# A decoder trunk on Trainium2: twelve input-projection tiles multiplied slice by slice in float32 beside the modulation, and S5 weights made in the same loop

## The chip, the cores and the metric

The kernel runs on one NeuronCore of a Trainium2 chip. The metric is the device time of one execution in microseconds; a change of it is read from medians over runs on the same chip.

## What is computed

A trunk of two layers over 256 tokens of width 2048. Only the start of a layer matters here: a modulation vector is made from the conditioning vector `c`, the input is normalised and modulated, and one wide projection feeds three groups of heads.

```python
for l in range(DEPTH):                     # DEPTH = 2
    mod = (silu(c) @ w_ada[l] + b_ada[l]).reshape(B, 6, D)
    sh1, sc1, gt1, sh2, sc2, gt2 = ...
    h = rmsnorm(x, g_pre_mix[l]) * (1.0 + sc1) + sh1
    proj = h @ w_in[l]                     # mLSTM, S5 and NSA inputs
    y = concat([mlstm(proj), s5(proj, lam, dt, b, c, d), nsa(proj)]) @ w_out[l]
    x = x + gt1 * rmsnorm(y, g_post_mix[l])
    h = rmsnorm(x, g_pre_ffn[l]) * (1.0 + sc2) + sh2
    x = x + gt2 * rmsnorm(conv_ffn(h), g_post_ffn[l])
```

The S5 group is a diagonal complex state space; its powers and mixing matrices are worked out on the chip from `lam`, `dt`, `b` and `c`, and applied as matrix products.

## The kernel before

The function `trunk` writes one program per engine: SyncE (SP) issues loads, GpSimd (POOL) issues other loads and does some vector work, TensorE (PE) multiplies, ScalarE (ACT) and VectorE (DVE) do the rest. Semaphores tie them. Tokens lie along the free dimension (256), features along the 128 partitions, so h is 16 slices of 128 features, and a projection tile is 128 output columns by 256 tokens.

**Head.** Shift and gain of layer 0's first modulation need 32 chunks of 1 MB of `w_ada` (16 for the shift, then 16 for the gain). SP issues them into five slots borrowed from three tensors (L455 to L460, `head_slot`); VectorE multiplies a chunk with silu(c) and sums it in one instruction (L1709 to L1716). Meanwhile x is loaded, normalised and turned. Twelve dummy matmuls (`keep`, HEAD_KEEP) run near the end of this. Only then come the modulated h, cut into a high and a low half, and the first two tiles (`first_proj`).

**Tiles.** 41 tiles follow in the order of ORDER: tiles 0 to 3 for S5, 4 to 15 keys and values, 16 the gates, 17 to 24 queries, 25 to 32 mLSTM, 33 to 40 values and output gates. Each needs two chunks of 512 KB, which SP loads into `ring`, a ring of five slots shared with other raw weights (compress weights at CMP_TILE, S5 tables at IN_TILE and OUT_TILE). Float32 accuracy is reached by three products of halves: ScalarE rounds a chunk (`w_head`, L1204 to L1206), VectorE subtracts it to get the rest (`w_rest`, L1652) and frees the slot (`raw_free`), and TensorE does 48 matmuls (`proj`, L671), after which ScalarE copies the tile out (`in_tile`, L1341).

```python
for p, (w, h) in enumerate(((w_hi, hT_hi), (w_hi, hT_lo), (w_lo, hT_hi))):
    m = pe.matmul(ps[:, bank, 0:SEQ], w[:, s, ks], h[:, k, :],
                  start=k == 0 and p == 0, stop=k == KT - 1 and p == 2)
```

**S5 weights.** Between the tiles VectorE makes the S5 weights of the layer: `s5_first`, `s5_second`, `s5_powers`, `s5_scaled`, then for each of four groups a block b (at tiles 6, 9, 12, 15, the tuple S5_B) and a block c one tile later. TensorE turns b (`s5_in_weights`) and multiplies c (`s5_own_weights`), and ScalarE sends three tables a group to DRAM (`s_in_w`, `s_out_w`, `s_own_w`); they come back through the ring from tile 18 on. From tile 15 on VectorE also multiplies half-chunks of the next modulation, which POOL loads into `ada_w`.

## Time and profile before

| what | value |
|---|---|
| time of three runs | median 2558.2 us (2551.77 to 2558.7) |
| the profiled execution | 2555.83 us, span 2553.9, granted clock 0.981 |
| busy | PE 2360.3 us (92%), weight loads 2056.5 (81%), DVE 1943.5 (76%), ACT 1304.7 (51%), POOL 262.5 (10%) |
| DMA | 643.07 MB, mean 252 GB/s |
| chain that ended last | PE 70%, DVE 17%, DMA 6%, ACT 4%, issue 2% |

The profile is of one execution. Busy times are sums over the whole span, and the chain is followed back from the last instruction, so its shares say which engine's work set the end. The stretch that the change rewrites is the first 187 us, and its rows are given further down.

### The profile page before, as it was taken

Reading aid. Unit: us, or ns where it says so; the run is one execution under the profiler, and the core shown is the slowest. Engines: PE = TensorE matmul, PEld = TensorE weight load, DVE = VectorE, ACT = ScalarE, POOL = GpSimd, SP = SyncE. Lnnn points to the kernel's source line nnn. Section 1 sums busy time; section 2 is a strip of 40 time slices with the busy share of each in tenths; the row PEclk is TensorE's granted clock in tenths of the full one; section 3 lists DMA queues with packets and bytes.
Section 4 is the critical chain, followed back from the end, with each engine's and each line's share of the span. In section 5 each row is a group of like instructions: output and inputs, shape, how many; then the busy total and the mean of one; then the engine's idle time right before and its main releaser. Section 6 shows DMA issues by size and latency. Waiting matters only on the chain.

```text
span 2553.9 us, 40347 instructions
## 1 busy us (share of the span) xinstructions
PE 2360.3 (92%) x14026; PEld 2056.5 (81%) x14026; DVE 1943.5 (76%) x2791; ACT 1304.7 (51%) x2089; POOL 262.5 (10%) x393
## 2 busy tenths in 40 slices
PE   1689779998999999999988999999899999999998
PEld 0589778766888888888878998887688888888886
DVE  7898887798999988867668976569897565565555
ACT  1565356546455454544448456654554544444444
POOL 0032311110111111100002121001010000000000
PEclk9999889999999999999999999999999999999999
DMA  9859767695999998868764675549596555556564
GB/s 396 328 195 322 268 248 252 221 358 204 354 344 341 334 338 325 318 230 276 263 243 149 226 249 186 141 145 367 207 353 238 184 186 188 183 188 189 190 194 152
DMA packets 187835, 643.07 MB, mean 252 GB/s; under 512 B 27249, under 2 KB 37617, under 8 KB 181697
## 3 DMA queue, kind: packets, MB, share of 16 engines
q1 hardware_dynamic: 120450, 455.28, 49.7%
q0 software_dynamic: 46656, 171.48, 19.5%
q10 hardware_dynamic: 20608, 14.72, 1.8%
q8 instruction: 74, 1.21, 0.2%
q14 instruction: 47, 0.39, 0.0%
HBM read 626.68 MB, written 14.71 MB: 251 GB/s over the span
## 4 chain that ended last, share of the span: by engine, by line
PE 70%; DVE 17%; DMA 6%; ACT 4%; issue 2%; ACTq 0%; SPq 0%; DVEq 0%; POOLq 0%
PE ps L1145 24%; PE ps L688 17%; PE ps L1146 12%; PE ps L671 8%; DVE w_lo L1652 5%; DMA ada_w<-ada_d 3%; DVE mix L1652 3%; DVE ada_w L1658 3%; PE ps L1025 2%; DMA ring<-stream 2%; ACT w_hi L1206 1%; DVE side L1652 1%; DVE mix L1658 1%; DVE mix L1655 1%; DMA s_own_w<-mix 1%
## 5 line engine op out<-in xcount | busy, mean ns | idle before, releaser
L1652 DVE TENSOR_TENSOR w_lo<-ring,w_hi 128x1024 fp32r<-128x1024 f32 x744 | 914.3, 1233 | 483.1 <-ACT w_hi L1206 480.1
L1206 ACT ACTIVATE w_hi<-ring 128x1024 fp32r<-128x1024 f32 x744 | 787.5, 1060 | 871.1 <-PE ps L1146 382.5
L1145 PE MATMUL ps<-hT,w_hi 128*128 128x512 f32 x2688 | 949.7, 399 | 0.5 <-DVE w_lo L1652 0.5
L1146 PE MATMUL ps<-hT,w_lo 128*128 128x256 f32 x2688 | 754.8, 281 | 0.0
L1145 PEld LDWEIGHTS ps<-hT,w_hi 128*128 128x128 f32 x2688 | 505.0, 188 | 126.9 <-DVE w_lo L1652 1.1
L1146 PEld LDWEIGHTS ps<-hT,w_lo 128*128 128x128 f32 x2688 | 507.8, 189 | 0.0
L671 PE MATMUL ps<-hT,w_hi 128*128 128x256 f32 x2496 | 474.7, 292 | 11.0 <-DVE w_lo L1652 11.0
L1658 DVE SCALAR_TENSOR_TENSOR ada_w<-ada_w,cs_row 128x1024 f32<-128x1024 f32 (+1 forms) x334 | 411.6, 1266 | 17.7 <-DMA ada_w<-ada_d 14.6
L671 PEld LDWEIGHTS ps<-hT,w_hi 128*128 128x128 f32 x2496 | 400.3, 197 | 22.7 <-issue 21.4
L671 PE MATMUL ps<-hT,w_lo 128*128 128x256 f32 x1248 | 358.4, 287 | 0.0
L671 PEld LDWEIGHTS ps<-hT,w_lo 128*128 128x128 f32 x1248 | 245.3, 197 | 0.0
L546 POOL DMA_DIRECT2D ada_w<-ada_d x256 | 135.2, 528 | 1067.7 <-DVE ada_w L1658 1062.9
L688 PE MATMUL ps<-w_hi,x_hi 128*128 128x512 f32 x656 | 202.3, 389 | 1.8 <-DVE x_lo L1652 1.8
L688 PE MATMUL ps<-w_hi,x_lo 128*128 128x512 f32 x656 | 202.0, 389 | 0.0
L688 PE MATMUL ps<-w_lo,x_hi 128*128 128x512 f32 x656 | 201.9, 389 | 0.0
L688 PEld LDWEIGHTS ps<-w_hi,x_hi 128*128 128x128 f32 x656 | 123.0, 188 | 27.9 <-DVE x_lo L1652 2.4
L688 PEld LDWEIGHTS ps<-w_lo,x_hi 128*128 128x128 f32 x656 | 123.1, 188 | 25.6
L688 PEld LDWEIGHTS ps<-w_hi,x_lo 128*128 128x128 f32 x656 | 123.1, 188 | 25.5
L636 PE MATMUL ps<-cst,mix 128*128 128x128 f32 x128 | 24.7, 374 | 97.1 <-ACT mix L1307 70.6
L636 PEld LDWEIGHTS ps<-cst,mix 128*128 128x128 f32 x128 | 22.6, 201 | 99.8 <-issue 70.7
L1658 DVE SCALAR_TENSOR_TENSOR mix<-ff_a,aux,mix 128x255 f32 (+3 forms) x172 | 82.8, 482 | 15.1 <-DVE mix L1658 12.2
L1025 PE MATMUL ps<-w_hi,x_hi 128*128 128x512 f32 x224 | 74.2, 413 | 13.5 <-DVE x_lo L1652 12.5
(292 smaller groups left out, 2324.8 us busy)
## 6 DMA issues: line engine op xcount, KB each, us to landing
ring<-stream SPq DMA_DIRECT2D x760, 512.0 KB, 4.4
ada_w<-ada_d POOLq DMA_DIRECT2D x320, 512.0 KB, 6.3
ada_w<-ada_d SPq DMA_DIRECT2D x14, 1024.0 KB, 10.0
ring<-ada_d SPq DMA_DIRECT2D x12, 1024.0 KB, 10.1
mix<-ada_d SPq DMA_DIRECT2D x6, 1024.0 KB, 10.2
xs<-x SPq DMA_DIRECT2D x2, 2048.0 KB, 11.9
s_in_w<-mix ACTq DMA_DIRECT2D x8, 512.0 KB, 3.4
s_out_w<-mix ACTq DMA_DIRECT2D x16, 256.0 KB, 6.6
```

The lines of the kernel that those rows point to most:

```text
L546: pool.dma_start(ada_w[:, s, :], ada_src(u * UG + j // 2, j % 2)).then_inc(ada_full[s], 16)
L636: m = pe.transpose(ps[:, b, k * SEQ + t * P:k * SEQ + (t + 1) * P], xn[:, t, (2 * b + k) * P:(2 * b + k + 1) * P], ident)
L671: m = pe.matmul(ps[:, bank, 0:SEQ], w[:, s, ks], h[:, k, :], start=k == 0 and p == 0, stop=k == KT - 1 and p == 2)
L688: m = pe.matmul(ps[:, 4 * t + 2 * half + b, :], xx[:, xs_, ts_], w[:, s, b * 512:(b + 1) * 512], start=k == 0 and p == 0, stop=False)
L1025: m = pe.matmul(ps[:, 4 * t + 2 * half + b, :], xx[:, j % 2, ts_], w[:, c % SPLIT, b * 512:(b + 1) * 512], start=j % KT == 0 and p == 0, s ...
L1145: pe.matmul(ps[:, bank, :], w_hi[:, s, ks], hT[:, k, :, :], start=k == 0, stop=False)
L1146: m = pe.matmul(ps[:, bank, SEQ:2 * SEQ], w_lo[:, s, ks], hT_hi[:, k, :], start=False, stop=k == KT - 1)
L1206: s.activation(w_hi[:, c % SPLIT, :], ring[:, at % RING, :], ACT.Copy).then_inc(hi_ready, 1)
L1652: return v.tensor_tensor(o, a, b, op)
L1655: return v.tensor_scalar(o, a, s1, s2, op0, op1)
L1658: return v.scalar_tensor_tensor(o, a, s, b, op0, op1, accum_out=total)
```

## The change

In layer 0 alone:

- POOL issues the 32 modulation chunks, into six slots (`ada_w` and the memory of `w_lo` and `w_hi`), shift and gain of a slice alternately, so that slice k of h is complete after chunk 2k + 1.
- SP loads x first, then the weights of tiles 0 to 11 as 24 chunks of 512 KB, each holding four tiles for two slices, in rows of 1 KB. They go through the ring of five slots and are freed by `head_used`.
- ScalarE makes slice k of h as soon as its two chunks are multiplied (`head_h`). TensorE multiplies it raw, in float32, with the twelve tiles of that slice (`head_products`), which are kept in six PSUM banks; all twelve end with slice 15. VectorE makes the low halves (`head_rest`) for the later tiles.
- The S5 weights are made between the chunks (HEAD_B, HEAD_C give the chunk numbers; HEAD_IN, HEAD_OWN the slices after which TensorE does its part), and ScalarE sends the tables after the `head_h` that follows.
- Tiles 12 on are as before, but the compress weights of layer 0 come at tiles 14 to 17, two a tile, instead of 10 to 17. The dummy matmuls, `first_proj` and the halves of tiles 0 to 11 are gone. Layer 1 does what it did.

```diff
-HEAD_UNITS, HEAD_SLOTS = 4, 5
-HEAD_X = 26
+HEAD_UNITS, HEAD_SLOTS = 4, 6
+HT, HW = 12, 4
+HG = HT // HW
+HF = 8
...
+CMP_AT = ([HT + 2 + i // 2 for i in range(N_CMP)], [CMP_TILE + i for i in range(N_CMP)])
...
+        def head_group(n):
+
+            return n // 2 + n % 2 * KT
 
         block = ctx.enter_context(nc.Block())
 
@@ -452,12 +473,7 @@
 
             sp.dma_start(c_row, c_cols.rearrange("(o p) k -> o (p k)", o=1)).then_inc(c_in, 16)
             sp.dma_start(cst[:, 0:K_FIRST], consts[:, 0:K_FIRST]).then_inc(cst_in, 16)
-            for n in range(HEAD_UNITS * UG):
-                if n >= HEAD_SLOTS:
-                    sp.wait_ge(ada_step, 2 * (n - HEAD_SLOTS + 1))
-                sp.dma_start(head_slot(n), ada_rows[n, :, :]).then_inc(head_full[n % HEAD_SLOTS], 16)
-                if n == 2 * HEAD_SLOTS:
-                    sp.dma_start(xs[:, :, :], x.rearrange("b (t p) d -> p (b t) d", p=P)).then_inc(x_in, 16)
+            sp.dma_start(xs[:, :, :], x.rearrange("b (t p) d -> p (b t) d", p=P)).then_inc(x_in, 16)
...
+            def head_src(c):
+
+                kp, g = divmod(c, HG)
+                at, col = C_IN + (ORDER[HW * g] - T_U) % NPROJ * 2, 2 * kp % KH * P
+                return stream[at:at + 2 * HW, :, :].rearrange("(t h) p n -> h p t n", h=2)[2 * kp // KH, :, :, col:col + 2 * P]
...
+            for n in range(HEAD_UNITS * UG):
+                if n >= HEAD_SLOTS:
+                    wait(ada_step, 2 * (n - HEAD_SLOTS + 1))
+                pool.dma_start(head_slot(n), ada_rows[head_group(n), :, :]).then_inc(head_full[n % HEAD_SLOTS], 16)
+                if n == HEAD_SLOTS - 1:
+                    pool.dma_start(cst[:, K_FIRST:], consts[:, K_FIRST:]).then_inc(cst_rest, 16)
...
+            def head_products(k):
+
+                h_hi.wait(pe, 0, k + 1)
+                for j in range(HT):
+                    c = HG * (k // 2) + j // HW
+                    at = RING_SPLIT[0][c]
+                    if k % 2 == 0 and j % HW == 0:
+                        pe.wait_ge(ring_full[at % RING], ring_count(0, at))
+                    bank, off = head_tile(0, j)
+                    o = j % HW * 2 * P + k % 2 * P
+                    m = pe.matmul(ps[:, bank, off:off + SEQ], ring[:, at % RING, o:o + P], h_f[:, k % HF, :],
+                                  start=k == 0 and j % 2 == 0, stop=k == KT - 1 and j % 2 == 1)
+                    if k == KT - 1:
+                        m.then_inc(w_used, 2)
+                    elif k % 2 and j % HW == HW - 1:
+                        m.then_inc(head_used, 1)
...
+                if l == 0:
+                    pe.wait_ge(xt_ready, 8)
+                    s5_b_transposes()
+                    for k in range(KT):
+                        head_products(k)
+                        if k in HEAD_IN:
+                            s5_in_weights(HEAD_IN.index(k))
+                        if k in HEAD_OWN:
+                            s5_own_weights(HEAD_OWN.index(k))
...
+                def head_h(k):
+
+                    s.wait_ge(ada_step, 4 * (k + 1))
+                    s.activation(sh_col[:, k:k + 1], head_sum[:, k:k + 1], ACT.Identity, bias=ada_b_c[:, k:k + 1]).then_inc(sh_ready, 1)
+                    s.activation(modA[:, k:k + 1], head_sum[:, KT + k:KT + k + 1], ACT.Identity, scale=A("g_pre_mix", k, k + 1),
+                                 bias=b_gain[:, k:k + 1]).then_inc(sh_ready, 1)
+                    if k >= HF:
+                        s.wait_ge(head_used, HG * ((k - HF) // 2 + 1))
+                        h_lo.wait(s, 0, (k - HF) // 2 + 1)
+                    s.wait_ge(sh_ready, 2 * (k + 1))
+                    s.activation(h_f[:, k % HF, :], xT[:, k, :], ACT.Identity, bias=sh_col[:, k:k + 1], scale=modA[:, k:k + 1])
+                    h_hi.by(s.activation(hT_hi[:, k, :], xT[:, k, :], ACT.Identity, bias=sh_col[:, k:k + 1], scale=modA[:, k:k + 1]))
...
+                    for k in range(KT):
+                        head_h(k)
+                        if k == 0:
+                            s5_b_columns()
+                        if k == 1:
+                            s5_skips()
+                        if k - 1 in HEAD_IN:
+                            in_weights(HEAD_IN.index(k - 1))
+                        if k - 1 in HEAD_OWN:
+                            out_weights(HEAD_OWN.index(k - 1))
+                            own_weights(HEAD_OWN.index(k - 1))
+                    for c in range(2 * HT, 2 * HT + AHEAD):
+                        w_head(c, used=False)
+                    for n in range(HT):
+                        if n == HF:
+                            h_lo.wait(s, l, 8)
+                        in_tile(n)
...
+                    for n in range(HEAD_UNITS * UG):
+                        head_chunk(n)
+                        if n == 2:
+                            for t in range(TT):
+                                rstd.wait(v, l, t + 1)
+                                v.reciprocal(stat[:, 4 + t:5 + t], stat[:, 2 + t:3 + t]).then_inc(x_root, 1)
+                        if n == 3:
+                            s5_first()
+                        if n == 7:
+                            s5_second()
+                        if n == 8:
+                            s5_powers()
+                        if n == 9:
+                            s5_scaled()
+                        if n >= 8 and n % 4 == 0:
+                            head_rest(n // 4 - 2)
+                        if n in HEAD_B:
+                            s5_weights_b(HEAD_B.index(n))
+                        if n in HEAD_C:
+                            s5_weights_c(HEAD_C.index(n))
+                    head_rest(6)
+                    head_rest(7)
+                    h_tmp.given += 8 - len(H_BY_ACT)
+                    v.sem_inc(h_tmp.sem, 8 - len(H_BY_ACT))
...
+HEAD_B, HEAD_C = (10, 15, 21, 26), (13, 19, 24, 29)
+HEAD_IN, HEAD_OWN = (6, 9, 11, 14), (8, 10, 13)
```

How the order of instructions changes, first on VectorE, around the S5 block c of the second group. `apow` are the S5 powers, `w_lo<-ring,w_hi` the low half of a weight chunk, `s5_own` TensorE's own-weights product and `st_out` the landed table. Before, between tiles:

```order
L1652 TENSOR_TENSOR w_lo<-ring,w_hi 128x1024 [waits hi_ready] x2
L1652 TENSOR_TENSOR mix<-aux,apow 128x640 [waits st_out,s5_own]
L1652 TENSOR_TENSOR side<-aux,apow 128x640 [waits dve]
L1652 TENSOR_TENSOR mix<-mix,side 128x640 [waits dve]
L1652 TENSOR_TENSOR mix<-aux,apow 128x640 [waits dve]
L1652 TENSOR_TENSOR side<-aux,apow 128x640 [waits dve]
L1652 TENSOR_TENSOR mix<-mix,side 128x640 [waits dve]
L1652 TENSOR_TENSOR w_lo<-ring,w_hi 128x1024 [waits hi_ready] x2
```

The block stands between the low halves of two tiles, and waits for `st_out` and `s5_own` there.

After, on the same engine, in the chunk loop (`ada_hi`, `ada_w`, `ada_lo` are slots of modulation chunks, `head_sum` their sums):

```order
L1792 SCALAR_TENSOR_TENSOR ada_hi,head_sum<-ada_hi,cs_row 128x2048 [waits head_full4]
L1786 TENSOR_TENSOR hT<-mix,hT 128x2x256 [waits h_hi]
L1792 SCALAR_TENSOR_TENSOR ada_hi,head_sum<-ada_hi,cs_row 128x2048 [waits head_full5]
L1792 SCALAR_TENSOR_TENSOR ada_w,head_sum<-ada_w,cs_row 128x2048 [waits head_full0]
L1792 SCALAR_TENSOR_TENSOR ada_w,head_sum<-ada_w,cs_row 128x2048 [waits head_full1]
L1786 TENSOR_TENSOR mix<-aux,apow 128x640 [waits st_out,s5_own]
L1786 TENSOR_TENSOR side<-aux,apow 128x640 [waits dve]
L1786 TENSOR_TENSOR mix<-mix,side 128x640 [waits dve]
L1786 TENSOR_TENSOR mix<-aux,apow 128x640 [waits dve]
L1786 TENSOR_TENSOR side<-aux,apow 128x640 [waits dve]
L1786 TENSOR_TENSOR mix<-mix,side 128x640 [waits dve]
L1792 SCALAR_TENSOR_TENSOR ada_lo,head_sum<-ada_lo,cs_row 128x2048 [waits head_full2]
```

The same block, with the same two waits, now stands in front of the remaining modulation chunks, and `hT` (the low half of h) among them.

ScalarE after, from slice 9 of h to the tables of the first group (`sh_col` and `modA` are the shift and gain of a slice):

```order
L1376 ACTIVATE sh_col<-head_sum,ada_b_c 128x1 [waits ada_step]
L1377 ACTIVATE modA<-head_sum,b_gain,aux 128x1
L1383 ACTIVATE mix<-mix,sh_col,modA 128x256 [waits sh_ready,h_lo,head_used]
L1384 ACTIVATE hT<-mix,sh_col,modA 128x256
L1477 DMA s_out_w<-mix 128x4x128 [waits s5_pow]
L1477 DMA s_out_w<-mix 128x4x128
L1489 ACTIVATE mix<-ps 32x4x32 [waits s5_zero,s5_own]
L1489 ACTIVATE mix<-ps 32x4x64
L1489 ACTIVATE mix<-ps 32x4x96
L1489 ACTIVATE mix<-ps 32x512
L1492 DMA s_own_w<-mix 128x512 [waits s5_own_ev]
```

The two issues of `s_out_w` and the own weights stand behind `head_h` of the next slice, which waits for its two chunks (`ada_step`), where before they stood behind a tile's evacuation.

The queue that issues the modulation chunks, before (SyncE, at the head):

```order
L453 DMA mix<-c_cols 1x2048
L454 DMA cst<-consts 128x261
L458 DMA ada_w<-ada_d 128x2048 x2
L458 DMA ring<-ada_d 128x2048 x2
L458 DMA mix<-ada_d 128x2048
L458 DMA ada_w<-ada_d 128x2048 [waits ada_step] x2
L458 DMA ring<-ada_d 128x2048 [waits ada_step] x2
L458 DMA mix<-ada_d 128x2048 [waits ada_step]
```

Each chunk behind the fifth waits for a multiplication (`ada_step`).

And after (POOL, which had only the small tables here before):

```order
L575 DMA posi<-pos 128x256
L576 DMA aux<-aux_d 128x64
L578 DMA mix<-ada_b 128x128
L579 DMA mix<-ada_b 64x128
L580 DMA aux<-aux_d 128x2642
L584 DMA ada_w<-ada_d 128x2048 x2
L584 DMA ada_lo<-ada_d 128x2048 x2
L584 DMA ada_hi<-ada_d 128x2048 x2
L586 DMA cst<-consts 128x1340
L584 DMA ada_w<-ada_d 128x2048 [waits ada_step,c_in] x2
```

The first chunk stands behind the tables and before the rest of the constants; the seventh waits for the first multiplication (`ada_step`).

SyncE now begins with x and the first five weight chunks, and its later loads up to tile 13 wait for TensorE (`head_used`, `w_used`).

## Rows read from the trace of the kernel before

In the windows view a row holds the stretch and its length, then busy us and count of PE, PEld, DVE, ACT and POOL, then the granted clock, the DMA share and GB/s. In the groups view: busy us, mean ns, then the idle time before them.

**Rows 1.** Windows view, three stretches of the start.
```profile
12.66:93.22 80.56, 10.08 (x51) 9.30 (x52) 72.87 (x66) 12.50 (x19) 1.09 (x2) 1.00 1.01 418
114.45:185.90 71.45, 64.36 (x539) 63.40 (x537) 63.40 (x101) 44.26 (x71) 21.24 (x20) 0.98 0.56 186
186.00:273.00 87.00, 74.36 (x692) 71.25 (x692) 71.06 (x88) 43.91 (x72) 16.62 (x18) 0.92 0.84 304
```

**Rows 2.** Chain of waits: start us, us, what; from 28, 114 and 245 us.
```profile
28.27 12.52 DMA ada_w<-ada_d
...
114.69 17.29 PE ps L671 x144
...
245.51 19.39 DMA s_own_w<-mix
```

**Rows 3.** DMA view, 12 to 80 us, total.
```profile
DMA packets 3890, 28.45 MB, mean 418 GB/s; under 512 B 417, under 2 KB 417, under 8 KB 417
```

**Rows 4.** Groups by form, 88 to 94 us: a chunk multiplication and the dummy matmuls.
```profile
L627 PE MATMUL ps<-cst 128*128 128x256 f32 x24 | 5.4, 383 | 1.4 <-DVE mix L1658 1.4
L1658 DVE SCALAR_TENSOR_TENSOR ada_w<-ada_w,cs_row 128x2048 f32<-128x2048 f32 x2 | 4.6, 2292 | 0.4 <-DMA ada_w<-ada_d 0.4
```

**Rows 5.** Timeline of PE, from 186 and from 273 us.
```profile
186.24 0.64 PE L817 MATMUL ps<-ring,side 128*32 128x128 f32 x16 [1.44 <-DMA ring<-stream]
...
273.04 0.58 PE L671 MATMUL ps<-hT,w_hi 128*128 128x256 f32 x1
```

**Rows 6.** Windows view: S5 first part, powers, scaled, a block b, a block c.
```profile
117.37:120.58 3.21, 3.21 (x29) 3.21 (x28) 2.76 (x18) 1.15 (x2) 0.00 (x0) 1.00 0.81 257
135.30:141.87 6.57, 6.57 (x57) 6.57 (x56) 5.89 (x21) 6.44 (x11) 2.56 (x2) 1.00 0.26 85
145.26:152.20 6.94, 3.99 (x34) 3.78 (x32) 6.77 (x7) 6.18 (x11) 6.54 (x8) 1.00 0.31 108
178.84:183.16 4.32, 4.32 (x38) 4.32 (x37) 4.15 (x8) 0.00 (x0) 0.00 (x0) 1.00 0.99 348
185.35:190.47 5.12, 4.23 (x46) 4.03 (x47) 4.95 (x8) 3.20 (x6) 0.00 (x0) 1.00 0.82 314
```

**Rows 7.** Groups by form, 93 to 300 us.
```profile
L1206 ACT ACTIVATE w_hi<-ring 128x1024 fp32r<-128x1024 f32 x52 | 55.2, 1062 | 50.9 <-DMA ring<-stream 29.8 <-PE ps L671 20.2 <-PE ps L656 0.8
...
L1287 ACT ACTIVATE hT<-ps,mod,modA 128x256 fp32r<-128x256 f32 x16 | 8.8, 611 | 0.0
...
L1652 DVE TENSOR_TENSOR hT<-mix,hT 128x512 fp32r<-128x512 f32 x8 | 5.3, 689 | 0.2
```

**Rows 8.** DMA view, 375.6 to 377.7 us: one load with 1 KB rows.
```profile
q1 hardware_dynamic: 528, 0.52, 80.2%
```

**Rows 9.** DMA view, 160 to 270 us: the queue of the S5 tables.
```profile
q10 hardware_dynamic: 5888, 5.24, 14.0%
```

**Rows 10.** View of the tile s_out_w, all executions of its issue.
```profile
DMA to landing us min/median/max: 2.7/5.8/20.1
```

**Rows 11.** The page, costliest groups and DMA issues (KB each, us to landing).
```profile
L546 POOL DMA_DIRECT2D ada_w<-ada_d x256 | 135.2, 528 | 1067.7 <-DVE ada_w L1658 1062.9
...
ring<-stream SPq DMA_DIRECT2D x760, 512.0 KB, 4.4
ada_w<-ada_d POOLq DMA_DIRECT2D x320, 512.0 KB, 6.3
```

**Rows 12.** Timeline of ACT: evacuations of tiles 17, 18 and 19.
```profile
231.21 0.38 ACT L1341 ACTIVATE mix<-ps 128x256 f32<-128x256 f32 x1
...
238.60 0.38 ACT L1341 ACTIVATE mix<-ps 128x256 f32<-128x256 f32 x1
...
249.22 0.38 ACT L1341 ACTIVATE mix<-ps 128x256 f32<-128x256 f32 x1
```

**Rows 13.** Windows view, just after the wait for s_own_w.
```profile
268.10:276.80 8.70, 8.66 (x39) 8.09 (x40) 8.60 (x10) 0.45 (x2) 2.63 (x4) 0.50 0.53 166
```

More of the change, by code:

```diff
@@ L110, in _ring_places @@
         for n in range(NRAW):
-            if min(2 * RAW_TILE[n] + 4, S_OUT - 1) == c:
+            if min(2 * tile[n] + 4, S_OUT - 1) == c:
                 raw.append(at)
@@ L387, in joint_parts, with raw, head_tile @@
             return slice(a, m), slice(m, D)
-        def raw(n):
-            return ring[:, RING_RAW[n] % RING, :]
+        def raw(l, n):
+            return ring[:, RING_RAW[l][n] % RING, :]
+        def head_tile(l, n):
+            return (n // 2, n % 2 * SEQ) if l == 0 and n < HT else (n % 2, 0)
         def modw(n):
@@ L1311, in _, with head_scaled, head_turned @@
-                h_evac(0, {4: 2, 6: 3} if l == 0 else {})
+                if l:
+                    h_evac(0, {})
+                def head_scaled(t):
+                    s.wait_ge(x_root, t + 1)
+                    for i in range(XN_PARTS):
+                        part = slice(i * D // XN_PARTS, (i + 1) * D // XN_PARTS)
+                        xn_ready.by(s.activation(xn[:, t, part], xs[:, t, part], ACT.Identity, scale=stat[:, 4 + t:5 + t]))
+                def head_turned(b):
+                    h_tr.wait(s, 0, b + 1)
+                    s.activation(xT[:, 2 * b:2 * b + 2, :].rearrange("p a b -> p (a b)"), ps[:, b, :], ACT.Copy
+                                 ).then_inc(xt_ready, 1)
```

333 lines of the change are left out of this document (185 added, 148 removed).

## Prediction

> **What bounds the kernel now.** I read the busy shares by stretch first, then the chain of waits, then the DMA view. In the first 93 us the DMA engines are full (share 1.01, 418 GB/s), while VectorE is busy 72.87 of 80.56 us and TensorE 10.08 [rows 1]. The chain says the same: each pair of modulation chunks is followed by some 10 us on the queue behind it [rows 2]. 28.45 MB went through in 68 us at 418 GB/s [rows 3], so a 1 MB chunk (1.049 MB) costs 2.51 us of DMA, and one multiplication on VectorE 2.29 us [rows 4]: the transfer bounds by a little. From 114 to 273 us VectorE (63.40 of 71.45, then 71.06 of 87.00) and TensorE (64.36, 74.36) share the stretch, and DMA has room [rows 1]. Tile 12 follows the raw matmuls that start at 186.24, and tile 21 starts at 273.04 [rows 5]. Between them lies one bare wait, 19.39 us for the S5 table `s_own_w`, written too shortly before [rows 2]. The change does the work up to tile 12 in another order; from tile 21 on the program is the same, so the question is when those two tiles begin.
>
> **The new head, on VectorE.** It now carries four things in one line, and I sum them.
> Start: x (2.1 MB), the large table (1.3 MB) and the first chunk must land, and the weight chunks queued beside them take about as much as the chunk and half of x; 5.5 MB at 418 GB/s [rows 3] is 13 us from issues at about 2: 15 (before, the first multiplication is at 12.66, where that stretch starts [rows 1]).
> Chunks: 32 × 2.29 = 73.3 [rows 4].
> S5 weights: the first part 3.2, powers 6.6, scaled 6.9, each b block 4.3, each c block 5.1 [rows 6]; the second part has 12 small operations against 18 in the first, 2.1; one memset 0.5. 3.2 + 2.1 + 6.6 + 6.9 + 0.5 + 4 × 4.3 + 4 × 5.1 = 56.9.
> Low halves of h: 8 × 0.69 = 5.5 [rows 7].
> Together 150.7. Against it stand the others. TensorE: 12 float32 matmuls of the slice's shape take 5.4 us (24 records) [rows 4], 16 slices 87, and at most 18 for the S5 transposes and own weights (20 matmuls a group, none dearer than these at 0.227). DMA: 32 × 2.51 = 80; a weight chunk now has 1 KB rows, and the one load of that kind took 80.2% of 2.1 us = 1.68 [rows 8], 24 of them 40; x and tables 10; S5 writes 14.0% of 110 us = 15 for four blocks, 11.5 for three [rows 9]. That is 142, below 151, so VectorE is the longest.
> Waits that the sum does not hold: early chunks that arrive late, 4 (the five weight loads stand in the same engines); and the S5 blocks. Block b of the second group waits for TensorE's transposes of the first, 4. Blocks c of groups two to four wait for `st_out`, the landing of the table of the group before. ScalarE issues it only behind `head_h` (two large activations of 0.61 [rows 7] and two small ones, 1.7), which itself waits for the chunk just multiplied. 1.7, two issues of about 0.5 and a landing between 2.7 and 5.8 [rows 10]: 5 to 8; I take 6, 5 and 7 for the three. Behind a c block on VectorE stand all later chunks, so this is paid in full, and the queue of chunks fills meanwhile for nothing. The bounds are 0 (all landed) and 20.1 each [rows 10]; I take the median since the DMA queues are far from full here. 150.7 + 4 + 4 + 18 = 176.7.
>
> **Chunks from POOL's queue.** Before, SP issued them; now POOL does, behind two small tables and the large one, with six slots. POOL's issues of the same tensor take 528 ns with VectorE beside them, and 512 KB lands 6.3 us later [rows 11]; six slots cover 5 × 5.5 = 27 us of the line on VectorE, so nothing is added. The Trainium skill speaks against the move: its page "SBUF — State Buffer" (section "SBUF: two separate sides") says that descriptors which GpSimd builds wait while VectorE holds the port that the two share; the 528 ns speak against it for these operations, and its outcome is a rival below.
>
> **From the head to tile 12.** After the last chunk: `head_h` 1.7. Then slice 15, which frees the three last weight slots; the loads of tiles 12 and 13 land 4.4 us after issue [rows 11], w_hi takes 1.06 twice [rows 7] and w_lo follows, while ScalarE also evacuates the first tiles. Slice 15 up to its first third 2, load 4.4, two w_hi and a w_lo 3.3, and 0.6 of issue: 10.3. Tile 12 starts at 176.7 + 12.0 = 189, where the raw matmuls before it started at 186.24 [rows 5]. So all the tile products taken out, and the splitting of their weights, buy nothing up to here: VectorE does nearly the same number of microseconds.
>
> **Tiles 12 to 20.** Before: 273.0 − 186.9 = 86, with the 19.39 in it. Now the S5 tables were written 20 us and more before they are loaded (own group four apart, at tile 12, loaded from tile 22 on). The wait goes. What is late next: two tiles without extra work at 5.8 (three tiles took 17.29 [rows 2]) and seven at the pace of 231.21 to 238.60, 7.4 [rows 12]; with the last own weights 3: 11.6 + 51.8 + 3.2 = 67. Eight compress chunks now come two per tile at tiles 14 to 17, in a ring of five; at 2.1 to 4.4 us a load I count them inside 7.4. Tile 21 starts at 189 + 67 = 256 against 273.0, gain 17. Removing the twelve dummy matmuls gives nothing, they hid behind the chunks. The modulation halves from tile 15 on are unchanged. Layer 1 is the same. The sum is against the profiled execution, 2555.8: **2539 us**. The median of the runs is 2.4 higher, so this is read with that much slack. A measurement here tells about 0.3% (7.7 us) from nothing.
>
> **Rivals.**
> *No waits in the head.* If the tables land in the shadow of a chunk, the 22 of waits and the 4 at the start vanish: 151, tile 12 at 160 with a shorter tail, tile 21 at 227, **2509**. For it: the writes are small and the DMA has room. Against: the order on ScalarE puts the issue behind the chunk after which VectorE asks.
> *The wait is only replaced.* The compress chunks take two of five slots each tile, every tile then waits for its weights as tile 18 to 19 did, 10.6 [rows 12]: 11.6 + 7 × 10.6 = 86, tile 21 at 275, **2558**.
> *Late filling.* Each of the six issues that fill the slots stands behind a VectorE operation as long as a chunk's, 6 × 2.29 = 14 later at the start: **2553**. This is where the rule of "SBUF — State Buffer" would lead. Against: POOL's issues last 528 ns [rows 11].
> *Slower: TensorE at half clock.* TensorE gets 5.4 us of work each 11 us. After the 19.39 us wait the granted clock was 0.50, the 1.2 GHz level, for 8.70 us, though it was busy [rows 13]. A slice at that level costs 10.9; from about 40 (x has to be scaled, turned and copied first) 16 × 10.9 = 174, S5 18, end 4: tile 12 at 236, tile 21 at 303, **2586**. It decides once a slice costs more than (177 − 40 − 18)/16 = 7.4. Against: a slice of 5.4 raises the clock again while it runs, then it costs between the two. The Trainium skill, "TensorE: Matmul & The Clock Gate" (section "HAM oscillation — how this bites in real kernels"), tells of a loop whose every burst starts slow because it waits before each; by that this rival would be nearer than I put it, and the row shows 0.50 after a far longer wait only.
> *Slower: the table writes land late.* At 19.4 each [rows 2] instead of 5.8, three times 13.6 = 41: **2580**. The writes have short rows and stand beside full queues of chunks, which speaks for it; the median speaks against.
>
> **Numbers.** Forecast 0.54, no waits 0.19, replaced 0.11, late filling 0.03, half clock 0.07, late landings 0.06. Faster: 0.52 of the forecast, 0.19, and 0.01 of the replaced wait, 0.72. Same: 0.02, 0.10 and 0.03, 0.15. Slower: 0.13. The range goes from 2506 (the first rival with 3 to spare) to 2562 (the replaced wait with 4); the two slow rivals, 0.13, stay out.
>
> **What would show it.** The first modulation multiply at about 15 and the last at about 177; the 128x640 group on VectorE preceded by waits on the `s_out_w` DMA of 5 to 7, three times; a slice's twelve matmuls in 5.4 at clock 1.00; tile 12 at 189, tile 21 at 256; no wait of 19 for `s_own_w`. Wrong it would be if TensorE's slices show clock 0.50 through the head, or if VectorE waits for chunks in the middle of it.

## The result and the profile after

The median of 20 runs is 2561.0 us against 2555.1 for the kernel before (20 runs); the ratio is 1.0031, with a 95% interval of 1.0016 to 1.0046. The change makes the kernel slower by 0.3%. The forecast was 2539 with a chance of 0.72 for faster. The direction was wrong, and that the median still lies in the forecast range is luck: tile 21 starts 30.9 us later than the sum has it, and the range was wide enough only because of a rival whose mechanism no run shows (below).

VectorE's timeline in the head: start us, us, operation, and in brackets the idle time before it and what ended it. The first multiplication, the first operation of each S5 block that waits, and the last multiplication:

```profile
16.65 2.29 DVE L1792 SCALAR_TENSOR_TENSOR ada_w<-ada_w,cs_row 128x2048 f32<-128x2048 f32 x1 [2.81 <-DMA ada_w<-ada_d]
...
94.71 0.69 DVE L1786 TENSOR_TENSOR mix<-aux,apow 128x512 f32<-128x512 f32 x1 [13.34 <-PE ps L792]
...
118.56 0.82 DVE L1786 TENSOR_TENSOR mix<-aux,apow 128x640 f32<-128x640 f32 x1 [10.08 <-DMA s_out_w<-mix]
...
149.33 0.82 DVE L1786 TENSOR_TENSOR mix<-aux,apow 128x640 f32<-128x640 f32 x1 [9.15 <-DMA s_out_w<-mix]
...
178.13 0.82 DVE L1786 TENSOR_TENSOR mix<-aux,apow 128x640 f32<-128x640 f32 x1 [7.79 <-DMA s_out_w<-mix]
...
185.38 2.29 DVE L1792 SCALAR_TENSOR_TENSOR ada_w<-ada_w,cs_row 128x2048 f32<-128x2048 f32 x1
```

The four waits that the forecast named are there, in the places it named, but they are 40.4 us and not 22. The last multiplication ends at 187.7, not 177.

Tile 12 and tile 21 on TensorE (the first and the last line, to be compared with [rows 5]), and between them the compress product that waits:

```profile
201.07 0.58 PE L693 MATMUL ps<-hT,w_hi 128*128 128x256 f32 x1 [3.96 <-ACT mix L1414]
...
233.72 1.08 PE L858 MATMUL ps<-ring,side 128*32 128x128 f32 x16 [4.55 <-DMA ring<-stream]
...
286.88 0.58 PE L693 MATMUL ps<-hT,w_hi 128*128 128x256 f32 x1
```

Tile 12 comes 12.1 us later than forecast and the nine tiles take 85.8 instead of 67, so tile 21 starts 13.8 us later than before. The long wait for `s_own_w` of [rows 2] is gone, as forecast, but nothing of its 19.39 us was gained: the nine tiles took 86.2 us before and take 85.8 now.

Windows view of the changed kernel, columns as in [rows 1]:

```profile
16.60:39.70 23.10, 7.84 (x43) 7.22 (x44) 19.55 (x34) 18.95 (x36) 3.70 (x7) 0.94 1.02 412
63.64:81.00 17.36, 17.36 (x72) 14.96 (x73) 17.16 (x18) 3.33 (x8) 2.11 (x4) 0.89 0.99 359
92.80:118.60 25.80, 19.86 (x91) 16.79 (x90) 13.64 (x16) 6.11 (x14) 2.11 (x4) 0.83 0.77 264
149.30:189.60 40.30, 21.49 (x104) 18.05 (x104) 30.73 (x35) 9.43 (x23) 0.53 (x1) 0.76 0.39 127
201.00:287.00 86.00, 75.66 (x645) 72.56 (x645) 59.24 (x61) 52.04 (x91) 37.99 (x38) 0.86 0.81 290
```

Up to 81 us the DMA engines are full (share 1.02 and 0.99); over the longer stretches behind that they are not (0.77 and 0.39). TensorE's granted clock is lower on average once its work comes in pieces (0.83, 0.76, 0.86, where the kernel before had 0.98 and 0.92 in [rows 1]). And GpSimd is busy 38 us in the last stretch against 16.6 before. The queues from 16 to 64 us (packets, MB, share of 16 engines):

```profile
q0 software_dynamic: 2285, 16.25, 82.3%
q1 hardware_dynamic: 3245, 3.22, 20.0%
```

Modulation chunks (q0) took four fifths of the DMA time, and the weights that TensorE waited for (q1) got 3.22 MB in 48 us.

### The profile page after: what moved, and what is told of

Same layout as the page of the kernel before. It is cut to its first block, busy times and chain, and to the rows that moved or that the text cites. A ratio compares the mean times of both kernels' runs of the same rounds, so it can differ in the third digit from the quotient of the medians.

```text
span 2557.1 us, 39914 instructions
## 1 busy us (share of the span) xinstructions
PE 2382.6 (93%) x13810; PEld 2069.2 (81%) x13810; DVE 1907.8 (75%) x2756; ACT 1297.5 (51%) x2116; POOL 278.7 (11%) x425
## 4 chain that ended last, share of the span: by engine, by line
PE 72%; DVE 14%; DMA 6%; ACT 5%; issue 2%; SPq 1%; ACTq 0%; DVEq 0%; POOLq 0%
PE ps L1202 24%; PE ps L710 17%; PE ps L1203 12%; PE ps L693 9%; DVE w_lo L1786 4%; DMA ring<-stream 3%; DVE ada_w L1792 3%; PE ps L1082 3%; DVE mix L1786 2%; ACT w_hi L1263 2%; PE ps L759 1%; DMA s_out_w<-mix 1%; DMA ada_w<-ada_d 1%; DVE side L1786 1%; DVE mix L1792 1%
## 5 line engine op out<-in xcount | busy, mean ns | idle before, releaser
L1786 DVE TENSOR_TENSOR w_lo<-ring,w_hi 128x1024 fp32r<-128x1024 f32 x720 | 888.7, 1238 | 493.3 <-ACT w_hi L1263 489.0
L1263 ACT ACTIVATE w_hi<-ring 128x1024 fp32r<-128x1024 f32 x720 | 761.3, 1059 | 837.1 <-PE ps L1203 348.2
L1203 PE MATMUL ps<-hT,w_lo 128*128 128x256 f32 x2688 | 753.8, 280 | 0.0
L1202 PEld LDWEIGHTS ps<-hT,w_hi 128*128 128x128 f32 x2688 | 504.1, 188 | 118.8 <-DVE w_lo L1786 0.9
L1203 PEld LDWEIGHTS ps<-hT,w_lo 128*128 128x128 f32 x2688 | 508.5, 189 | 0.0
L693 PE MATMUL ps<-hT,w_hi 128*128 128x256 f32 x2176 | 418.2, 294 | 9.4 <-DVE w_lo L1786 5.5
L693 PEld LDWEIGHTS ps<-hT,w_hi 128*128 128x128 f32 x2176 | 352.5, 199 | 20.9 <-issue 15.0
L693 PE MATMUL ps<-hT,w_lo 128*128 128x256 f32 x1088 | 314.2, 289 | 0.0
L693 PEld LDWEIGHTS ps<-hT,w_lo 128*128 128x128 f32 x1088 | 215.5, 198 | 0.0
L710 PE MATMUL ps<-w_hi,x_hi 128*128 128x512 f32 x656 | 202.4, 390 | 1.8 <-DVE x_lo L1786 1.8
L759 PE MATMUL ps<-mix,ring 128*128 128x256 f32 x384 | 102.9, 434 | 48.9 <-ACT hT L1384 38.7
L759 PEld LDWEIGHTS ps<-mix,ring 128*128 128x128 f32 x384 | 83.5, 221 | 66.1 <-ACT hT L1384 31.6
L1792 DVE SCALAR_TENSOR_TENSOR mix<-ff_a,aux,mix 128x255 f32 (+3 forms) x172 | 82.9, 482 | 15.1 <-DVE mix L1792 12.2
L1731 ACT ACTIVATE mix<-ff_a,aux 128x256 f32 (+1 forms) x86 | 51.1, 594 | 75.2 <-DVE ff_a L1786 75.0
## 6 DMA issues: line engine op xcount, KB each, us to landing
ada_w<-ada_d POOLq DMA_DIRECT2D x12, 1024.0 KB, 10.4
ada_lo<-ada_d POOLq DMA_DIRECT2D x10, 1024.0 KB, 11.6
```

The costliest lines, as they stand in the source:

```text
L693: m = pe.matmul(ps[:, bank, 0:SEQ], w[:, s, ks], h[:, k, :], start=k == 0 and p == 0, stop=k == KT - 1 and p == 2)
L710: m = pe.matmul(ps[:, 4 * t + 2 * half + b, :], xx[:, xs_, ts_], w[:, s, b * 512:(b + 1) * 512], start=k == 0 and p == 0, stop=False)
L759: m = pe.matmul(ps[:, bank, off:off + SEQ], ring[:, at % RING, o:o + P], h_f[:, k % HF, :], start=k == 0 and j % 2 == 0, stop=k == KT - 1 ...
L1202: pe.matmul(ps[:, bank, :], w_hi[:, s, ks], hT[:, k, :, :], start=k == 0, stop=False)
L1203: m = pe.matmul(ps[:, bank, SEQ:2 * SEQ], w_lo[:, s, ks], hT_hi[:, k, :], start=False, stop=k == KT - 1)
L1263: s.activation(w_hi[:, c % SPLIT, :], ring[:, at % RING, :], ACT.Copy).then_inc(hi_ready, 1)
```

## The experiments

All times of tiles and chunks are from one profile of each kernel; ratios are to the kernel before on the same chip, with 95% intervals. Two profiles of one and the same kernel differ by 0.3 to 1.6 us at tile 12 and by 1.5 to 1.8 at tile 21 (the last experiment), so smaller differences between two kernels say nothing.

**Tables issued earlier (a_out).**

```diff
+                        if k in HEAD_OUT:
+                            out_weights(HEAD_OUT.index(k))
                         if k - 1 in HEAD_OWN:
-                            out_weights(HEAD_OWN.index(k - 1))
...
+HEAD_OUT = (7, 10, 12)
```

> The two issues of s_out_w move ahead of the own weights and up to two slices earlier on ScalarE (behind head_h of slices 7, 10 and 12). Theory 1 (VectorE's c blocks wait for the landing of that table, 10.1, 9.2 and 7.8 us in the changed kernel): the second and third wait nearly vanish, the first falls only to the end of TensorE's own weights (some 2 us less, since slice 8 ends late), so the last chunk ends some 11 to 14 us earlier than 187.6 and tile 12 starts at about 188. Rival (the landing only looks last, the blocks wait for TensorE's own weights all the same): waits stay at 8 to 10, last chunk within 3 us of 187.6. Whole time 10 lower, or unchanged.

Ratio 0.9990 (0.9965 to 1.0014). The last chunk ends at 182.2 and tile 12 starts at 195.3. Waits view of VectorE, head (total us, times, longest):

```profile
DVE mix L1787 <- PE ps L792: 14.3, 1, 14.3
DVE mix L1787 <- PE ps L810: 12.4, 2, 7.9
DVE mix L1787 <- DMA s_out_w<-mix: 8.4, 1, 8.4
```

The last chunk ends 5.5 us earlier, half of what was expected. Two of the three waits for the table now end with TensorE's own weights (L810), 7.9 and 4.4, which the table had hidden; the third is still for the table. So both theories hold in part: the issue order costs 5.5 us, and behind it stands TensorE. In this profile both passes of the up projection are of the shorter kind described in the last experiment.

**Second b block later (b_late).**

```diff
-HEAD_B, HEAD_C = (10, 15, 21, 26), (13, 19, 24, 29)
+HEAD_B, HEAD_C = (10, 17, 21, 26), (13, 19, 24, 29)
```

> Block b of the second group comes after chunk 17 and not after chunk 15. Theory 1 (it waits 13.3 us for TensorE, which is behind because its weight chunks arrive late, while modulation chunks lie ready in the slots): VectorE multiplies two more chunks in that time, its wait falls from 13.3 to about 8, last chunk about 5 us earlier, unless the first c block waits longer in its place. Rival (the DMA queues are full until 92 us, so nothing that VectorE does earlier helps): the wait shrinks but the same time comes back as a wait for chunks or in the next blocks; last chunk still at 187 within 2.

Ratio 1.0031 (1.0009 to 1.0053). The wait shrinks from 13.3 to 12.2 only, the last chunk ends at 187.3, tile 12 starts at 201.0: the rival. TensorE's transposes end 3.9 us later (98.6 against 94.7), and TensorE waits 14.7 us for its weights in the head where it waited 10.2, so the two chunks that VectorE does ahead of them gain nothing.

**Contiguous weight rows (e_rows).** The rows are 4 KB instead of 1 KB. This multiplies other weights in tiles 0 to 11, so the output is not the trunk's; the work is the same.

```diff
-                return stream[at:at + 2 * HW, :, :].rearrange("(t h) p n -> h p t n", h=2)[2 * kp // KH, :, :, col:col + 2 * P]
+                return stream[c, :, :].rearrange("p (t n) -> p t n", t=HW)
```

> The 24 weight chunks of tiles 0 to 11 are read as contiguous chunks with 4 KB rows and not as 1 KB rows; this multiplies other weights, so tiles 0 to 11 hold other numbers (the work is the same). Theory 1 (1 KB packets take turns with 8 KB packets of the modulation chunks and so get a small share while those stream): TensorE's waits for the ring in the head (10 us in three waits, and the wait before slice 0) go, slices 0 to 6 end before 80 us and block b of the second group waits 4 instead of 13.3; last chunk about 9 us earlier. Rival (the DMA is simply full, 418 GB/s, whatever the rows): TensorE's waits stay, last chunk within 3 us of 187.6.

Ratio 1.0006 (0.9981 to 1.0031). VectorE's waits in the head:

```profile
DVE mix L1786 <- DMA s_out_w<-mix: 33.6, 3, 14.0
DVE ada_w L1792 <- DMA ada_w<-ada_d: 6.1, 2, 4.7
```

The wait for TensorE's transposes (13.3) is gone altogether, so late weights had made it, and with 4 KB rows they are hardly late (TensorE waits 1.8 us for the ring and not 10.2). But the waits for the table grew from 27.0 to 33.6, and only 3.7 us reach tile 12 (197.3). Up to 64 us the weights got no more than before (3.38 MB against 3.22); from 64 to 78 us they got 1.86 MB against 1.27, and the transposes end at 83.5 and not 94.7.

**Both moves (c_both).**

```diff
+HEAD_B, HEAD_C = (10, 17, 23, 27), (13, 20, 25, 30)
+HEAD_IN, HEAD_OWN = (6, 9, 12, 14), (8, 11, 13)
+HEAD_OUT = (7, 10, 12)
```

> Both moves together: tables issued early, second b block after chunk 17, third after 23, fourth after 27, c blocks after 13, 20, 25 and 30, TensorE's parts moved with them. Theory 1 (the four waits of VectorE, 40.4 us in all, are set by TensorE's lateness and the issue order): they fall to 10 or less, the last chunk ends at 157 to 162, tile 12 starts at about 173, and the whole is 15 to 28 us below the changed kernel, so clearly below the kernel before. Rival (the waits move to the modulation chunks or to TensorE, whose slices then bound): last chunk at 175 or later, whole within 8 of the changed kernel.

Ratio 0.9965 (0.9941 to 0.9989), median 2544.4: below the kernel before, and 1.0031 to 0.9965 is 17 us. So the waits in the head decided the direction. Both passes of the up projection in its profile take 475 us (see the last experiment), as in the kernel before, and still a span of 2546.7 us against 2553.9. The last chunk ends at 170.2 and not at 157 to 162, tile 12 starts at 182.5. Two long waits are left, 13.1 for TensorE's transposes and 8.4 for a table whose two writes, issued at 122.5 and 123.0, had landed at 141.2: together 21.5 where theory 1 had 10 or less. It is theory 1 in the main, with less than it promised.

**First b group turned earlier (g_early).** As before, with

```diff
+HEAD_B, HEAD_C = (10, 17, 23, 27), (13, 20, 26, 30)
+HEAD_IN, HEAD_OWN = (5, 9, 12, 14), (8, 11, 13)
+HEAD_OUT = (7, 10, 13)
```

> Like the run with both moves, but TensorE turns the first b group after slice 5 and not after slice 6, and the third c block comes after chunk 26. Theory 1 (VectorE's 13.1 us there are TensorE waiting for the weight chunks of slices 6 and 7, which the modulation chunks crowd out): the wait goes and VectorE works on; last chunk at 157 to 161 instead of 170.2. Rival (the DMA queues are full until 92 us, so VectorE then waits for modulation chunks or for ScalarE in the next block): last chunk at 166 to 171. Whole 8 to 12 us lower than the run with both moves, or within 4 of it.

Ratio 0.9938 (0.9904 to 0.9973), median 2540.9 of five runs; the interval overlaps that of c_both, and its one profile starts tile 12 later than c_both's (185.4 against 182.5). The waits view:

```profile
DVE mix L1787 <- PE ps L810: 17.1, 1, 17.1
DVE mix L1787 <- DMA s_out_w<-mix: 9.0, 1, 9.0
```

The 13 us went and came back as 17 at the next block that needs TensorE; the last chunk ends at 173.1, where theory 1 had 157 to 161 and the rival 166 to 171. So the rival's kind of outcome came, but the wait moved to TensorE and not to chunks or ScalarE. TensorE is late as a whole there, not in one place.

**Contiguous rows on top (j_rows).** This is g_early with the edit of e_rows, so tiles 0 to 11 hold other numbers again.

> The kernel with the earlier first b group, with the weight chunks of tiles 0 to 11 read contiguously (4 KB rows; other weights, so tiles 0 to 11 hold other numbers, same work). Theory 1 (what is left of VectorE's waits there, 17.1 us for TensorE's own weights of group one, is late weight chunks in 1 KB packets): the wait falls to 5 or less, the last chunk ends at 158 to 163 instead of 173.1. Rival (TensorE itself, its clock and its place in the order, makes that wait): it stays above 10, last chunk at 168 or later.

Ratio 0.9962 (0.9945 to 0.9979).

```profile
DVE mix L1787 <- DMA s_out_w<-mix: 21.7, 2, 13.4
...
DVE ada_lo L1793 <- DMA ada_lo<-ada_d: 2.8, 2, 1.5
```

TensorE's own weights of group one are done at 100 us, 14 earlier, so the part of theory 1 on the rows holds; but the block then waits 13.4 for the first table, issued at 84.7 and 85.1. The view of that table's writes, all of them in the run (the longest is this one):

```profile
DMA to landing us min/median/max: 2.6/4.7/28.8
```

The last chunk ends at 171.6 and not at 158 to 163. Taking one wait away shows the next: at this one block it was 17.1 us for TensorE and is 13.4 for the table.

**Blocks moved two or three chunks further (m_best).**

```diff
+HEAD_B, HEAD_C = (10, 17, 24, 28), (13, 22, 27, 31)
+HEAD_IN, HEAD_OWN = (5, 9, 12, 14), (8, 11, 13)
+HEAD_OUT = (7, 11, 13)
```

> The kernel with the earlier first b group, with the second c block after chunk 22 and not 20, the third after 27, the fourth after the last chunk, the third and fourth b blocks after 24 and 28. Theory 1 (VectorE's 17.1 and 9.0 us there are waits for work that would be done anyway two or three chunks later): both shrink below 5, the last chunk ends at 152 to 160 instead of 173.1, and tile 12 starts 10 to 18 us earlier than 185.4. Rival (slices on TensorE and the DMA queues bound the head by now): the waits move to the chunks or to slice 15, tile 12 within 5 us of 185.4.

Ratio 0.9957 (0.9941 to 0.9974), median 2546.8. The last chunk ends at 165.8 and tile 12 starts at 181.2, 4.2 earlier than in g_early; one c block now comes behind the last chunk. The 17 us stay (17.3), only later, and the 9.0 for the table falls to 4.6: the rival in the main. TensorE waits 20.1 us for its weights in the head here, 21.7 in g_early. The three versions c_both, g_early and m_best beat both kernels, and these runs don't tell which of them is best.

**Filler on TensorE (f_fill, h_fill).** Eight matmuls by zeros behind each of slices 6 to 14, and eight behind slice 15, on the changed kernel and on g_early.

```diff
+                        if 6 <= k < KT - 1:
+                            for _ in range(8):
+                                pe.matmul(ps[:, 0, 0:SEQ], nul[:, :], cst[:, 0:SEQ], start=False, stop=False)
...
+                    for _ in range(8):
+                        pe.matmul(ps[:, 7, 0:SEQ], nul[:, :], cst[:, 0:SEQ], start=True, stop=True)
```

> The changed kernel with eight matmuls by a zero tile (3.6 us at full clock, they add nothing) behind each slice from 6 to 14 and eight behind slice 15. Theory 1 (TensorE falls to the 0.50 clock in the gaps between slices, and slices 8, 10, 12, 15 and tile 12 run 1.3 to 3 us long): granted clock in 92 to 190 us rises from about 0.8 to above 0.95, these slices take 5.5, tile 12 takes 6.0 and starts 2 to 4 us earlier than 201. Rival (the clock is off the path, the filler only stands in front of the S5 products that VectorE waits for): tile 12 starts at 201 or later by up to 5.

> The previous kernel with the zero matmuls. Theory 1: with the waits of VectorE gone TensorE's slices are closer together and matter more, so the filler brings 3 to 6 us up to tile 12. Rival: TensorE is now nearly full (16 slices of 5.5 and the S5 products from 40 us on), and the filler delays it: tile 12 3 to 10 us later than without.

Windows of h_fill, and of g_early for the same stretches:

```profile
92.00:150.00 58.00, 56.92 (x286) 49.80 (x287) 31.86 (x36) 11.16 (x26) 4.22 (x8) 0.97 0.82 304
150.00:190.00 40.00, 38.99 (x207) 34.22 (x206) 28.72 (x32) 14.69 (x31) 0.00 (x0) 1.00 0.44 141
```

```profile
92.00:150.00 58.00, 45.62 (x216) 38.03 (x216) 31.50 (x36) 11.03 (x26) 4.22 (x8) 0.88 0.83 303
150.00:190.00 40.00, 27.02 (x130) 23.27 (x131) 28.80 (x32) 17.70 (x39) 1.65 (x2) 0.83 0.51 172
```

The clock does rise (0.88 and 0.83 to 0.97 and 1.00; from 0.82 and 0.76 to 0.92 and 0.91 on the changed kernel), tile 12 takes 6.0 us instead of 7.3 and 7.5, and it brings nothing: tile 12 starts at 202.8 and 188.5, 1.7 and 3.1 later than without, the 1.7 being hardly more than two profiles of one kernel differ by. By tile 21 the two are even with their bases (285.7 against 286.9, 273.3 against 273.1). The ratios are 1.0043 (1.0019 to 1.0067) and 1.0003 (0.9982 to 1.0024). So the filler costs about as much as the clock gives: the rivals.

**Compress chunks spread (i_cmp), on g_early.** The first product now also waits until the twelve tiles are copied out.

```diff
+CMP_AT = ([HT + 1, HT + 1, HT + 2, HT + 3, HT + 3, HT + 4, HT + 4, HT + 5], [CMP_TILE + i for i in range(N_CMP)])
```

> The kernel with the earlier first b group, and the eight compress chunks at tiles 13, 13, 14, 15, 15, 16, 16, 17 and not two at each of 14 to 17. Theory 1 (two extra loads per tile in a ring of five make TensorE and ScalarE wait for the ring: 4.6 us before the compress of tile 16 and the drop of the clock behind it): that wait falls below 1.5, and tiles 12 to 20 take 79 or less where they took 83 to 86. Rival (the stretch is bound by ScalarE's evacuations, the S5 table loads and the clock): 83 to 86 again.

Ratio 0.9994 (0.9973 to 1.0014). Tile 12 at 188.1 to tile 21 at 277.2 is 89.1, g_early has 87.7: the rival's outcome. It is a weak test: the chunks move by one tile at most, and a product now waited 8.6 us for ScalarE instead.

**Half-chunks of the next modulation later (k_ada), on g_early.**

```diff
-ADA_SLOT = 15
+ADA_SLOT = 20
```

> The kernel with the earlier first b group; the half-chunks of the next modulation begin at tile 20 and not at tile 15 (denser afterwards). Theory 1 (tiles 14 to 20 are short of DMA: two compress loads a tile, the tiles' own, the half-chunks and the S5 tables, share 0.98 and 1.01 there): tile 21 starts 6 to 12 us after tile 12 sooner than the 87.7 us of the base, the loads land in about 4 and not 6 us; part of it comes back behind tile 21. Rival (five ring slots freed late by ScalarE and VectorE bound it, not the transfer): 84 to 90 again.

Tile 12 to tile 21 is 186.6 to 265.6, 79.0 instead of 87.7, and the loads of the S5 tables land in 4.4 instead of 7.8 us. The amount is theory 1's, but the run does not show that DMA alone is the cause: it takes 6.3 MB of loads out of the stretch, and with them the 14 half-chunk multiplications of 1.22 us on VectorE, some of which are in the chain that ends at tile 21 (3.52 us of it, shown below for the changed kernel). The ratio is 0.9981 (0.9965 to 0.9997) against 0.9938 (0.9904 to 0.9973), so nothing of the 8.7 us is seen in the whole: the up projection, which follows the mixer, starts at 627.5 against 618.0. The half-chunks have to be done somewhere, and in these two profiles they cost more there.

**GpSimd's preparation of the compress blocks left out (l_noblk), on g_early.** The eight additions that fill the blocks are left out in layer 0, so the blocks are zero there and the output is not the trunk's.

```diff
-                    pool.memset(blk_all[:, kv, :, 2 * NC:CW], 0.0)
-                    for h in range(NKV):
+                    if l == 0:
+                        b = pool.memset(blk_all[:, kv, :, :], 0.0)
+                    else:
+                        pool.memset(blk_all[:, kv, :, 2 * NC:CW], 0.0)
+                    for h in range(NKV if l else 0):
```

> The kernel with the earlier first b group, leaving out in layer 0 the eight additions on GpSimd that prepare the compress blocks (they become zero). Theory 1 (GpSimd's work, which now comes in one piece behind the twelve evacuations, slows VectorE's operations beside it: 2.26 us for a low half against 1.23): the low halves in the first 25 us behind tile 12 take 1.3 to 1.6 us, and tile 21 starts 4 to 8 us earlier after tile 12. Rival (the slow operations are off the path there): the operations are faster, but tile 21 starts within 2 us of the 87.7 after tile 12.

Groups of VectorE's low halves from 185 to 215 us, in g_early and then in this kernel:

```profile
L1787 DVE TENSOR_TENSOR w_lo<-ring,w_hi 128x1024 fp32r<-128x1024 f32 x7 | 12.9, 1867 | 9.3 <-ACT w_hi L1263 9.3
```

```profile
L1790 DVE TENSOR_TENSOR w_lo<-ring,w_hi 128x1024 fp32r<-128x1024 f32 x7 | 9.8, 1403 | 15.1 <-ACT w_hi L1266 15.1
```

Tile 12 to tile 21 takes 78.1 (186.6 to 264.7), 9.6 less than in g_early, and the up projection starts 7.8 earlier (610.2 against 618.0). The low halves there are 3.1 us shorter together (12.9 to 9.8), and VectorE's other operations in those 30 us 4.3 (10.4 to 6.1). That is theory 1, and more than it promised; how the rest comes about was not tried. The step from tile 15 to tile 16 alone falls from 14.6 us to 7.2, with the same compress loads. Ratio 0.9949 (0.9926 to 0.9971), whose interval does not separate it from g_early's: the profile shows the gain, the medians don't.

**Both kernels once more (after_again, before_again).**

> The changed kernel once more, for a second profile. Theory 1 (a pass of the up projection takes 466 or 475 us by the execution, whatever the kernel, and hides or adds 9 us each time): its head is within 1 us of the first profile at tile 12 (201.1) and tile 21 (286.9), while one of the two passes may differ by 8.7. Rival (the faster first pass belongs to the changed kernel): first pass 466 again, second 475 again.

> The kernel before once more, for a second profile. Theory 1: tile 21 at 273 within 1, and at least one pass of the up projection may take 466 where both took 475. Rival: both 475 again.

The matmuls of the up projection from 700 to 900 us, in the first profile of the changed kernel and in the second:

```profile
L1202 PE MATMUL ps<-hT,w_hi 128*128 128x512 f32 x578 | 200.4, 391 | 0.0
```

```profile
L1202 PE MATMUL ps<-hT,w_hi 128*128 128x512 f32 x568 | 200.7, 399 | 0.0
```

Tile 12 is at 200.8 and tile 21 at 285.4 in the second profile, within 0.3 and 1.5 us of the first: the head repeats, a little less closely at tile 21 than expected. The first pass of the up projection took 466.2 us in the first profile and 475.9 in the second (from the start of its first matmul to the start of its last), of the same kernel. So one program can have either, by the execution: theory 1 for the changed kernel. In the kernel before all four passes of the two profiles took 475, the outcome that its rival named; tile 12 was at 186.8 and 188.4 and tile 21 at 273.0 and 274.9. Whether the kernel before ever has the faster pass is not shown: in the other 14 profiles 8 of 28 passes were of that kind, and with such a share four of 475 in a row are no surprise. The spans of the second profiles are 2564.9 and 2561.2.

## Why the prediction was wrong, step by step

**Start.** Forecast 15, measured 16.65. The rival of a late filling did not occur: POOL's issues take 0.53 us in the head too. I had drawn this rival from "SBUF — State Buffer" of the Trainium skill (section "SBUF: two separate sides") too widely. The section has the building of descriptors locked out while VectorE runs an operation in a two-port mode; an operation with two SBUF inputs it sets only against GpSimd operations that read SBUF. The chunk multiplications have two SBUF inputs, so its rule does not lead to this rival, and the issues beside them took no longer than elsewhere.

**VectorE's own work.** Forecast 73.3 + 56.9 + 5.5 = 135.7; measured 187.7 − 16.65, less 40.4 and 3 of small waits for chunks, 127.6. It was 8 too dear. The S5 weights took 52.3 instead of 56.9, the chunks 71.2 instead of 73.3 (back to back one begins 2.21 us after the other), and two of the eight low halves of h come behind the last chunk. Nearly all that the S5 weights saved is in two steps whose rows had GpSimd beside them [rows 6]: the powers took 6.6 with GpSimd busy 2.56 us and now take 4.4, the scaled step took 6.9 with GpSimd busy 6.54 and now takes 4.3:

```profile
53.25 2.87 DVE L1786 TENSOR_TENSOR mix<-aux,s5p 128x512 f32<-128x512 f32 x4
...
56.15 0.69 DVE L1786 TENSOR_TENSOR aux<-mix 128x512 f32<-128x512 f32 x1
56.88 0.69 DVE L1792 SCALAR_TENSOR_TENSOR aux<-mix 128x512 f32<-128x512 f32 x1
```

**Waits in the head: this step failed.** The mechanism was named rightly, the sizes not. (a) "Block b of the second group waits for TensorE's transposes of the first, 4" was 13.3. The DMA sum (142 in 177 us) was used as an average; up to 81 us the engines are full, and from 16 to 64 us the packets of the chunks' queue took 82.3% of their time. TensorE waited for the ring at 54.7, 63.6 and 90.3 us (10.2 in all) and began the transposes at 92.8 only; e_rows takes that wait away. (b) "6, 5 and 7" for the tables were 10.1, 9.2 and 7.8. A c block waits for both writes of a table, and the second write of the three landed 8.8, 10.6 and 6.5 us after its issue. The landing had been taken at 5.8, the median over both writes and both layers, "since the DMA queues are far from full here". That premise was wrong. The windows view of the three landings, with the DMA share in the last column but one:

```profile
109.65:118.47 8.82, 8.82 (x51) 7.51 (x50) 0.00 (x0) 2.35 (x6) 0.00 (x0) 0.87 0.84 326
138.59:149.23 10.64, 8.35 (x56) 7.41 (x56) 1.58 (x3) 2.28 (x6) 0.53 (x1) 1.00 1.03 368
171.56:178.04 6.48, 6.48 (x45) 5.65 (x45) 0.00 (x0) 2.29 (x6) 0.00 (x0) 1.00 0.98 300
```

The slots that VectorE has just freed are refilled beside the first two (64.3% and 70.1% of the engines' time for the chunks' queue), weights beside the third (62.2%). The kernel before could have told: the second writes of its four groups in layer 0 landed after 6.7, 6.6, 12.4 and 20.1 us. (a) and (b) are together 40.4 us instead of 22, which minus the 8 above and with the later start gives 187.7 instead of 177. c_both, which shortens them to 21.5, is faster than the kernel before.

**From the last chunk to tile 12.** 13.4 instead of 12.0: slice 15 ran 7.5 us and not 5.4, at a granted clock of 0.74 from 187 to 201 us, behind 8.6 us of idle TensorE. This is the rival of the half clock, and it came in part. Four slices from 92 us on followed 5.9, 7.9, 11.6 and 8.6 us of idle TensorE, and took 8.4, 8.0, 7.7 and 7.5 us at a mean granted clock of 0.64 to 0.72, between the levels of 1.2 and 2.4 GHz; slices that followed on work took 5.3 to 5.5 at 0.97 to 1.00. "TensorE: Matmul & The Clock Gate" of the Trainium skill (section "HAM oscillation — how this bites in real kernels") tells of a loop whose every burst starts slow because it waits before each, and for the four slices the trace agrees. It is worth 2 to 3 us in such a slice, and these four are as long as the 7.4 us from which the prediction let the clock decide; but TensorE was idle before each of them, waiting for h, and f_fill, which raises the clock, brings tile 12 no earlier. So it did not bound the head.

**Tiles 12 to 20: this step failed most.** 85.8 instead of 67. I counted nine tiles at the pace of the kernel before and took the wait of 19.39 off; the sum had no term for the work that the first twelve tiles hand on to GpSimd. The rival "the wait is only replaced" gave 86, but that is luck: it had the compress loads as the cause, and l_noblk has the same loads and takes 78.1. What filled the place is read from the chain of waits of the changed kernel (start us, us, what), between tiles 12 and 21:

```profile
219.42 6.71 DVE w_lo L1786 x3
...
226.52 9.80 DMA ring<-stream
...
256.08 5.46 DMA ring<-s_in_w
...
275.80 3.52 DVE ada_w L1792 x6
```

(a) GpSimd's work. Rotations and compress blocks of twelve tiles became due at once (GpSimd busy 38 us, 16.6 before), and VectorE beside it slowed; its low halves free the ring slots late, and the load behind them holds up the compress product and the tile behind it. l_noblk gets 9.6 back. (b) The half-chunks of the next modulation, whose loads stand beside those of the S5 tables and whose multiplications stand on VectorE: k_ada gets 8.7 back, and does not tell the two apart. (a) and (b) overlap in tiles 18 and 19, so they are not a sum. (c) The clock was lower too, 0.86 against 0.92; what that costs in these tiles was not tried by itself.

**Behind tile 21** the program was taken as unchanged, and it is. From tile 21 to the end it took 2280.9 and 2286.4 us in the two profiles of the kernel before, 2270.2 and 2279.5 in those of the changed one. Without the two passes of the up projection, counted to the end of their last matmul, that is 1330.3 and 1335.2 against 1328.3 and 1327.9. So in the profiles tile 21 is 12.2 us later on average and the rest a little shorter, which fits the smaller difference of the medians, 5.9 us; what makes the rest shorter is open, and two profiles of each are too few to say that it is.

Measured against its own sum: 12.1 late at tile 12, 18.8 more up to tile 21, so 286.9 for 256. With the rest as long as in the first profile of the kernel before, this would be 2570 us, outside the range.

## What to carry to other kernels

Where an engine's line holds waits for others, don't add them up at median landings taken over a whole run: look at what fills the DMA engines while that very transfer is under way, and which of several writes ends the wait. Work that is gathered (twelve tiles that end together) hands the next engine its work in one piece: ask what then falls due on the engines that were never on the path, and whether a busy neighbour was in the row from which a duration is taken. And a wait that is removed by moving its producer is worth only the distance to what stands behind it; here late weights, TensorE's own work and the landing of a table stood close behind one another.
